# Latent attention entry: the last gate product behind three key and query tiles, its weights in a spent sum buffer, the key rotation on GpSimd, SiLUs ahead of the exponentials

## Chip, cores and metric

One Trainium2 chip, one of its NeuronCores. The metric is device time in microseconds (us) of one execution. The engines are named as in the profile: PE is TensorE, DVE is VectorE, ACT is ScalarE, POOL is GpSimd, SP is SyncE, which issues most transfers here.

## What is computed

Two layers on x of 512 tokens by 1024 columns, fp32. The first, which the change touches, is multi-head latent attention with a gate; the second is a sparse attention.

```
proj = rms_norm(x) @ w_in               # 1024 -> 384 + 256 + 64 + 2048
c_q, c_kv, k_pe, z = split(proj)
q  = rms_norm(c_q) @ w_uq               # 16 heads of 192
kv = rms_norm(c_kv) @ w_ukv             # 16 heads of 128 + 128
k  = concat(k_pe (shared), k_nope)
q, k = rope(rms_norm(q)), rope(rms_norm(k))    # first 64 columns rotate
o  = causal_attention(q, k, v)
x  = x + (o * silu(z)) @ w_out
```

## The kernel before

Each fp32 matmul is three fp32r ones: an operand is split into a high part (a copy by ACT, `w_hi`) and a low part (the difference, by DVE or POOL, `w_lo`), and PE forms hi·hi, lo·hi and hi·lo (`mm3`, L95 to L97). A PE weight tile can be used when both parts are there.

The five engines run written-out programs in order and meet only at semaphores, so each engine's order is exactly the order of its code.

**Gate products.** The gate path z (2048 columns) is computed in four chunks of 512 columns, each by seven half-size products in place of eight (sums of blocks on both sides, Strassen's scheme). They are numbered 0 to 27 here (`NB` = 28); product i is seven-step q = i // 7, block b = i % 7. For each, ACT makes `w_hi` (`block_hi`), DVE `w_lo` (`block_lo`, L1896) in a ring of four half buffers, PE runs 24 matmuls of 256 columns (`z_product`), and DVE adds the bank into z (`z_sums`). Some blocks are differences that DVE makes first (`w_difference`, L1912). ACT applies SiLU to the finished quarters (`z_leave`). The token side of blocks 1 to 3 are sums of h, in three buffers `h_sum`; each is last read by product 22, 23 or 24.

**Key rotation.** In the loop step after product 17 or so (`p == 18`), DVE scales and rotates the shared 64 key columns of all tokens (`keys_rotate`, L1960): eight small instructions, of which the last counts `kpe_step` to 4. SP waits for that before it loads the first head weights.

**Entry into the heads.** A tile is 128 tokens. `project_kv(m)` (6 matmuls of 256 columns) and `project_q(m)` (9 of 384) make keys with values, and queries of two heads, for tile m. The first head weights lie where ring places of products 24 and 25 were, the second where those of 26 and 27 were; they are split by `split_kv` and `split_q` on ACT and then DVE. PE's order is products 0 to 26, `project_kv(0)`, `project_q(0)`, product 27, then the slots.

**Slots.** From then on all engines run `step(s)` for s = -7 to 65. Slot s of PE holds `scores(s)`, `turn(s + 4)` (four transposes of normed keys and queries), `project_kv(s + 8)`, `values(s - 2)`, `turn_probs(s - 1)`, and a `project_q` in each of slots -8 to -5 and in every second slot from -2 on. Before tile m is turned, ACT squares it (`q_stats`, `kv_stats`), POOL makes the factors by a power (`k_factor`, `q_factor`), DVE scales (`scale_k`, `scale_q`) and rotates the first three tiles, POOL rotates the others (`rotate`). After it, ACT copies the high part (`high`) and DVE subtracts (`low`), which frees the bank (`x_free`). POOL first clears two parts of `qkT_lo`, after `z_used` has reached 28. In slot 0, ACT runs the first `exponential` and then the last pair of SiLUs.

## Time and profile before

| | |
|---|---|
| median of 3 runs | 944.73 us (943.12 to 945.89) |
| profiled execution, first to last instruction | 944.0 us |
| PE busy | 920.2 us (97%) |
| DVE, ACT, POOL busy | 557.2, 447.6, 413.8 us |

The profiled execution's time is given by its span alone. In the page PE is busy nearly all the time, so the idle time of the other engines matters only where PE waits for them, and the place to look is where PE is not busy.

### The profile page before, as it was taken

The page shows a single profiled execution, that of the slowest core. Times are in us where ns is not written, and L with a number is a line of the kernel's source. Part 1 is how long each engine was busy: PE and PEld are TensorE (multiplying, and loading weights), DVE is VectorE, ACT ScalarE, POOL GpSimd, SP SyncE. Part 2 cuts the span into 40 slices and gives each one's busy share as a digit, 9 for nine tenths or more (in the row PEclk, how much of TensorE's full clock was granted, in tenths as well). Part 3 has the DMA queues.
Part 4 walks back from the last instruction along what each step waited for, and adds up shares of the span by engine and source line. Part 5 has one row for each costly group of instructions (what it writes and reads, how often), then busy time and mean ns, then how long its engine had stood idle before and what let it go on. Part 6 is the DMA issues. An engine that isn't in the chain of part 4 may idle for free.

```text
span 944.0 us, 16372 instructions
## 1 busy us (share of the span) xinstructions
PE 920.2 (97%) x5910; PEld 824.9 (87%) x5910; DVE 557.2 (59%) x1665; ACT 447.6 (47%) x1019; POOL 413.8 (44%) x589
## 2 busy tenths in 40 slices
PE   6999997999999999999999999999999999999998
PEld 6999987999999998888888887888888999999986
DVE  5898867887788877211111125676946666666611
ACT  5456556877777777222342233444344333333310
POOL 2000118888888884133373335666713111111021
PEclk9999999999999999999999999999999999999999
DMA  6322412101111011213272122222120100000011
GB/s 203 116 90 90 126 38 92 49 12 49 48 39 48 24 47 47 86 50 120 84 155 104 58 76 89 90 95 88 53 84 5 42 1 1 1 1 1 2 38 52
DMA packets 39322, 58.91 MB, mean 62 GB/s; under 512 B 8757, under 2 KB 22346, under 8 KB 39242
## 3 DMA queue, kind: packets, MB, share of 16 engines
q1 hardware_dynamic: 39200, 57.85, 19.2%
q8 instruction: 48, 0.79, 0.3%
q14 instruction: 32, 0.26, 0.1%
q10 hardware_dynamic: 42, 0.01, 0.0%
HBM read 55.63 MB, written 2.10 MB: 61 GB/s over the span
## 4 chain that ended last, share of the span: by engine, by line
PE 81%; ACT 1%; DVE 0%; issue 0%; DVEq 0%
PE bank L95 16%; PE bank L96 15%; PE bank L97 15%; PE bank L533 7%; PE bank L1113 4%; PE bank L453 2%; PE bank L462 2%; PE bank L454 2%; PE bank L431 2%; PE bank L1102 2%; PE bank L1074 1%; PE bank L1075 1%; PE bank L1093 1%; PE bank L1092 1%; PE bank L469 1%; PE bank L518 1%
## 5 line engine op out<-in xcount | busy, mean ns | idle before, releaser
L1769 POOL TENSOR_TENSOR w_lo<-w_raw,w_hi 128x2048 fp32r<-128x2048 f32 (+1 forms) x26 | 118.3, 4549 | 148.6 <-ACT w_hi L1520 148.5
L95 PE MATMUL bank<-w_hi,h_hi 128*128 128x512 f32 (+3 forms) x480 | 172.9, 360 | 1.2 <-DVE h_lo L1816 0.9
L97 PE MATMUL bank<-w_hi,h_lo 128*128 128x512 f32 (+3 forms) x480 | 169.1, 352 | 0.0
L96 PE MATMUL bank<-w_lo,h_hi 128*128 128x512 f32 (+3 forms) x480 | 169.1, 352 | 0.0
L95 PEld LDWEIGHTS bank<-w_hi,h_hi 128*128 128x128 f32 x480 | 90.7, 189 | 13.9 <-issue 2.5
L97 PEld LDWEIGHTS bank<-w_hi,h_lo 128*128 128x128 f32 x480 | 90.6, 189 | 11.5
L96 PEld LDWEIGHTS bank<-w_lo,h_hi 128*128 128x128 f32 x480 | 90.7, 189 | 10.1
L1520 ACT ACTIVATE w_hi<-w_raw 128x2048 fp32r<-128x2048 f32 (+1 forms) x26 | 49.2, 1891 | 76.7 <-PE bank L97 76.7
L692 POOL TENSOR_TENSOR o_c<-o_c,o_sw 128x256 f32<-128x256 f32 x16 | 11.6, 727 | 167.2 <-DVE o_c L766 167.2
L533 PE MATMUL bank<-kvr,probT 128*128 128x65 f32 x640 | 80.7, 273 | 0.0
L95 PE MATMUL bank<-w_hi,c_hi 128*128 128x256 f32 (+1 forms) x224 | 76.9, 343 | 3.3 <-DVE w_lo L1991 0.9
L533 PEld LDWEIGHTS bank<-kvr,probT 128*128 128x128 f32 x640 | 78.6, 192 | 1.3
L95 PE MATMUL bank<-w_hi,o_hi 128*128 128x512 f32 x192 | 77.3, 403 | 0.0
L96 PE MATMUL bank<-w_lo,o_hi 128*128 128x512 f32 x192 | 75.8, 395 | 0.0
L97 PE MATMUL bank<-w_hi,o_lo 128*128 128x512 f32 x192 | 75.7, 394 | 0.0
L97 PE MATMUL bank<-w_hi,c_lo 128*128 128x256 f32 (+1 forms) x224 | 69.5, 310 | 0.0
L96 PE MATMUL bank<-w_lo,c_hi 128*128 128x256 f32 (+1 forms) x224 | 69.3, 309 | 0.0
L717 DVE CUSTOM_DVE_ANT_0 scored<-bank,band 128x128 f32<-128x128 f32 (+3 forms) x128 | 56.4, 487 | 18.6 <-PE bank L431 18.6
L636 ACT ACTIVATE probT<-bank 128x512 f32<-128x512 f32 (+1 forms) x96 | 47.0, 524 | 30.0 <-PE bank L469 29.1
L1470 ACT ACTIVATE qkT_hi<-bank 128x512 fp32r<-128x512 f32 x64 | 38.3, 599 | 30.9 <-PE bank L1075 30.8
L1730 POOL TENSOR_TENSOR ms_k<-ms_k,minus_half 128x1 f32<-128x1 f32 x64 | 46.0, 719 | 5.3
L1113 PE MATMUL bank<-kv_sb,probT 128*128 128x128 f32 x320 | 46.5, 276 | 1.3 <-DVE probT L2052 0.9
(312 smaller groups left out, 2390.0 us busy)
## 6 DMA issues: line engine op xcount, KB each, us to landing
w_raw<-in_nsa_w_in SPq DMA_DIRECT2D x10, 1024.0 KB, 4.9
w_raw<-in_mla_w_in SPq DMA_DIRECT2D x8, 1024.0 KB, 5.0
w_raw<-in_mla_w_out SPq DMA_DIRECT2D x8, 1024.0 KB, 5.0
w_raw<-in_nsa_w_in SPq DMA_DIRECT2D x8, 984.0 KB, 4.9
w_raw<-in_nsa_w_out SPq DMA_DIRECT2D x4, 1024.0 KB, 5.0
w_raw<-in_mla_w_uq SPq DMA_DIRECT2D x7, 576.0 KB, 4.1
w_raw<-in_mla_w_ukv SPq DMA_DIRECT2D x15, 256.0 KB, 2.6
w_raw<-in_mla_w_in SPq DMA_DIRECT2D x4, 704.0 KB, 5.7
```

The costliest lines, as they stand in the source:

```text
L95: nc.tensor.matmul(out, a[0], b[0], start=start, stop=False)
L96: nc.tensor.matmul(out, a[0], b[1], start=False, stop=False)
L97: return nc.tensor.matmul(out, a[1], b[0], start=False, stop=stop)
L431: nc.tensor.matmul(first_bank(k)[:, 0:nb * keys].rearrange("p (b c) -> p b c", b=nb), qT_hi[a][0:DK, tok], kT_hi[0:DK, b0:b0 + nb, n // HP ...
L533: last = nc.tensor.matmul(o_most[:, i, b, :] if i < 3 else o_last[:, b, :], probT[n % 2][:, at:at + P], kvr[:, j, c0:c0 + DV1], start=j == ...
L636: nc.scalar.activation(probT[n % 2][:, at:at + wide], score_bank[k % 3][:, 0:wide], ACT.Exp).then_inc(exp_done, 1)
L717: last = nc.vector.tensor_tensor_reduce(scored[k % 2][:, w * keys:(w + 1) * keys], first_bank(k)[:, w * keys:(w + 1) * keys], band[:, SEQ ...
L1113: last = nc.tensor.matmul(o_bank[:, 0:DV0], probT[:, i % 2, j * P:(j + 1) * P], kv_sb[:, h % 4 * NT + j, NOPE:WKV], start=j == 0, stop=j == i)
L1470: nc.scalar.activation(qkT_hi[m // NT % 2][:, :, t * P:(t + 1) * P], x_bank[m % 2][:, :].rearrange("p (a t) -> p a t", a=4), ACT.Copy).the ...
L1520: nc.scalar.activation(w_hi[g % 2][:, :, 0:width], w_raw[g % 2][:, :, 0:width], ACT.Copy).then_inc(m_hi, 1)
L1730: nc.gpsimd.tensor_tensor(at, at, minus_half[:, 0:1], ALU.pow).then_inc(k_factors, 1)
L1769: nc.gpsimd.tensor_tensor(w_lo[g % 2][:, :, 0:width], w_raw[g % 2][:, :, 0:width], w_hi[g % 2][:, :, 0:width].bitcast(F32), ALU.subtract). ...
```

## The change

Five edits, all around the entry.

- Product 27 runs after `project_kv` and `project_q` of tiles 0, 1 and 2. Its weights go into `h_sum[2]`, which product 24 was the last to read, and its result into bank 7; the first turn into bank 7, `turn(1)`, waits for its sum. The second head weights can then be split after product 26 in place of 27.
- `keys_rotate` moves from DVE to POOL, behind POOL's work on the latent factors.
- POOL clears `qkT_lo` after `z_used` has reached 23, not 28.
- ACT and DVE split the first head weights ahead of the SiLUs and sums of products 25 and later.
- The last SiLUs are run in slot -4, and a one-column Exp on a spare tile in slot -3 loads the Exp table there.

```diff
-z_bank = lambda i: bank[i % 4 if i < NB - 2 else (3, 2)[i - NB + 2]]
-bank_user = lambda i: i - 4 if i < NB - 2 else i - (3, 5)[i - NB + 2]
+z_bank = lambda i: bank[i % 4 if i < NB - 2 else (3, 7)[i - NB + 2]]
+bank_user = lambda i: i - 4 if i < NB - 2 else i - 3
+z_hi_at = lambda i: in_ring(w_hi, i) if i < NB - 1 else h_sum[2][0][:, :, :]
+z_lo_at = lambda i: in_ring(w_lo, i) if i < NB - 1 else h_sum[2][1][:, :, :]
...
 def turn(m):
+    if m == 1:
+        pe.wait_ge(z_sum, Z_STEPS * NZ)
...
 # PE
-    for q in range(NZ):
-        for b in range(7):
-            if 7 * q + b == NB - 1:
-                project_kv(0)
-                project_q(0)
-            z_product(q, b)
-    slots(step, KV0 + 1)
+    for i in range(NB - 1):
+        z_product(i // 7, i % 7)
+    project_kv(0)
+    project_q(0)
+    step(KV0 + 1)
+    step(KV0 + 2)
+    z_product(NZ - 1, 6)
+    slots(step, KV0 + 3)
...
 # ACT, split_q and split_kv
-    act.wait_ge(z_used, NB - 2 + 2 * p)
+    act.wait_ge(z_used, NB - 2 + p)
 # ACT, step
-    if s == 0:
+    if s == KV0 + 1:
+        z_leave(NB - 2)
+    if s == T0:
         z_leave(NB - 1)
+    if s == T0 + 1:
+        nc.scalar.activation(exp_junk[:, 0:1], minus_half[:, 0:1], ACT.Exp)
...
 # POOL
+    pool.wait_ge(gains_loaded, 16 * 6)
+    pool.wait_ge(tables_done, 1)
+    keys_rotate()
     pool.wait_ge(kpe_step, 4)
-    pool.wait_ge(z_used, NB)
+    pool.wait_ge(z_used, NB - 5)
...
 # DVE, after the loop over p
+    z_sums(NB - 4)
+    split_kv(0)
+    split_q(0)
+    z_sums(NB - 3)
+    z_sums(NB - 2)
+    split_kv(1)
+    block_lo(NB - 1)
+    split_q(1)
```

First place, PE at the entry. Each row shown begins one group (`c_hi` as input: a projection, 256 columns for keys, 384 for queries; `h_hi` as input: product 27). Before:

```order
L95 MATMUL bank5<-w_hi0,c_hi_57 128x256 [waits c_lo_made,wk_ready]
...
L95 MATMUL bank4<-w_hi0,c_hi_57 128x384 [waits c_lo_made,wq_ready]
...
L95 MATMUL bank2<-w_hi1,h_hi_68 128x256 [waits z_sum,z_lo]
...
L95 MATMUL bank1<-w_hi0,c_hi_57 128x256 [waits z_sum]
...
L95 MATMUL bank0<-w_hi0,c_hi_57 128x384 [waits z_sum]
...
L95 MATMUL bank5<-w_hi0,c_hi_57 128x256 [waits kv_out]
...
L95 MATMUL bank3<-w_hi0,c_hi_57 128x384 [waits z_sum]
...
L95 MATMUL bank1<-w_hi0,c_hi_57 128x256 [waits kv_out]
...
L95 MATMUL bank2<-w_hi0,c_hi_57 128x384 [waits z_sum]
...
L1074 MATMUL bank6<-ident,qn_70 128x128 [waits k_scaled,k_rotated,q_rotated]
```

and after:

```order
L95 MATMUL bank5<-w_hi0,c_hi_57 128x256 [waits c_lo_made,wk_ready]
...
L95 MATMUL bank4<-w_hi0,c_hi_57 128x384 [waits c_lo_made,wq_ready]
...
L95 MATMUL bank1<-w_hi0,c_hi_57 128x256 [waits z_sum]
...
L95 MATMUL bank0<-w_hi0,c_hi_57 128x384 [waits z_sum]
...
L95 MATMUL bank5<-w_hi0,c_hi_57 128x256 [waits kv_out]
...
L95 MATMUL bank3<-w_hi0,c_hi_57 128x384 [waits z_sum]
...
L95 MATMUL bank7<-h_sum_hi2_91,h_hi_69 128x256 [waits z_lo]
...
L95 MATMUL bank1<-w_hi0,c_hi_57 128x256 [waits kv_out]
...
L1079 MATMUL bank6<-ident,qn_71 128x128 [waits k_scaled,k_rotated,q_rotated]
```

Product 27 moved behind the projections of tiles 1 and 2, and reads `h_sum_hi` in place of the ring.

Second place, DVE at the entry (bank into `z_sb`: a sum; `w_lo0<-wh_first`: the first head weights; `w_lo1<-w_raw0`: the second). Before:

```order
L1928 TENSOR_TENSOR z_sb_56<-bank0,z_sb_56 128x2x256 [waits z_sum,z_used]
...
L1931 TENSOR_TENSOR z_sb_56<-bank1,z_sb_56 128x2x256 [waits z_used]
L1991 TENSOR_TENSOR w_lo0<-wh_first_97,w_hi0 128x512 [waits wk_hi_made]
L1986 TENSOR_TENSOR w_lo0<-wh_first_97,w_hi0 128x1152 [waits wq_hi_made]
L1934 TENSOR_TENSOR z_sb_56<-bank3,z_sb_56 128x2x256 [waits z_sum,z_used]
L1937 TENSOR_TENSOR z_sb_56<-bank2,z_sb_56 128x2x256 [waits z_sum,z_used]
...
L1991 TENSOR_TENSOR w_lo1<-w_raw0,w_hi1 128x512 [waits wk_hi_made,o_free]
L1986 TENSOR_TENSOR w_lo1<-w_raw0,w_hi1 128x1152 [waits wq_hi_made]
L2023 SCALAR_TENSOR_TENSOR kn_102<-kv_sb_71,ms_k_67,gk0 128x128 [waits k_factors,kv_out]
```

and after:

```order
L1958 TENSOR_TENSOR z_sb_56<-bank0,z_sb_56 128x2x256 [waits z_sum,z_used]
...
L2005 TENSOR_TENSOR w_lo0<-wh_first_98,w_hi0 128x512 [waits wk_hi_made]
L2000 TENSOR_TENSOR w_lo0<-wh_first_98,w_hi0 128x1152 [waits wq_hi_made]
L1961 TENSOR_TENSOR z_sb_56<-bank1,z_sb_56 128x2x256 [waits z_used]
L1964 TENSOR_TENSOR z_sb_56<-bank3,z_sb_56 128x2x256 [waits z_sum,z_used]
L2005 TENSOR_TENSOR w_lo1<-w_raw0,w_hi1 128x512 [waits wk_hi_made]
L1926 TENSOR_TENSOR h_sum_lo2_92<-w_diff_97,h_sum_hi2_91 128x1024 [waits z_hi]
L2000 TENSOR_TENSOR w_lo1<-w_raw0,w_hi1 128x1152 [waits wq_hi_made]
...
L2037 SCALAR_TENSOR_TENSOR kn_103<-kv_sb_72,ms_k_67,gk0 128x128 [waits k_factors,kv_out,o_free]
```

Both splits of the first head weights moved ahead of one sum, and those of the second ahead of tile 0's scaling but without the wait for product 27, whose own split stands between them.

Third place, ACT around the first exponential (`below` as input). Before:

```order
L1478 ACT_TABLE_LOAD
L1478 ACTIVATE prob_107,rowsum_64<-below0_105,negmax_63 128x128 [waits max_done]
L1378 ACT_TABLE_LOAD
L1378 ACTIVATE z_sb_56<-z_sb_56,ms_x_61 128x256 [waits z_sum]
...
L1470 ACTIVATE qkT_hi1_99<-bank7 128x4x128 [waits x_done]
...
L1478 ACT_TABLE_LOAD
L1478 ACTIVATE prob_107,rowsum_64<-below1_106,negmax_63 128x256 [waits max_done]
```

and after:

```order
L1384 ACTIVATE z_sb_56<-z_sb_56,ms_x_61 128x256 [waits z_sum]
...
L1476 ACTIVATE qkT_hi0_99<-bank7 128x4x128 [waits x_done]
...
L1514 ACT_TABLE_LOAD
L1514 ACTIVATE exp_junk_68<-minus_half 128x1
L1476 ACTIVATE qkT_hi0_99<-bank6 128x4x128 [waits x_done]
...
L1484 ACTIVATE prob_108,rowsum_64<-below0_106,negmax_63 128x128 [waits max_done]
...
L1476 ACTIVATE qkT_hi1_100<-bank7 128x4x128 [waits x_done]
...
L1484 ACTIVATE prob_108,rowsum_64<-below1_107,negmax_63 128x256 [waits max_done]
```

Of three table loads one is left, two turns further ahead, and the SiLUs stand before it.

## Rows read from the trace of the kernel before

**Rows 1.** Page, part 1: busy us, share of the span, instructions.
```profile
PE 920.2 (97%) x5910; PEld 824.9 (87%) x5910; DVE 557.2 (59%) x1665; ACT 447.6 (47%) x1019; POOL 413.8 (44%) x589
```

**Rows 2.** Stretches: busy (count) of PE, PEld, DVE, ACT, POOL; PEclk, DMA, GB/s.
```profile
132.00:136.00 4.00, 4.00 (x19) 4.00 (x19) 0.00 (x0) 2.21 (x9) 0.00 (x0) 0.58 0.00 0
...
152.00:156.00 4.00, 4.00 (x20) 3.90 (x18) 1.75 (x6) 2.13 (x7) 3.65 (x10) 0.57 0.00 2
...
172.00:229.00 57.00, 57.00 (x435) 55.79 (x434) 45.81 (x154) 44.09 (x148) 48.91 (x112) 1.00 0.13 40
```

**Rows 3.** Waits of PE from 172 us on: us in total, times, longest.
```profile
PE bank L1113 <- DVE probT L2052: 0.9, 2, 0.7
```

**Rows 4.** Timeline of PE, gate products: start, us, instruction, [idle before <-releaser].
```profile
112.81 0.39 PE L95 MATMUL bank<-w_hi,h_sum_hi 128*128 128x256 f32 x1 [0.23 <-DVE w_lo L1896]
...
119.90 0.39 PE L95 MATMUL bank<-w_hi,h_sum_hi 128*128 128x256 f32 x1 [0.44 <-DVE w_lo L1896]
```

**Rows 5.** Timeline of PE, entry into the heads.
```profile
129.65 0.39 PE L95 MATMUL bank<-w_hi,c_hi 128*128 128x256 f32 x1 [0.95 <-DVE w_lo L1991]
...
131.37 0.44 PE L95 MATMUL bank<-w_hi,c_hi 128*128 128x384 f32 x1 [0.75 <-DVE w_lo L1986]
...
132.07 0.52 PE L95 MATMUL bank<-w_hi,c_hi 128*128 128x384 f32 x1
...
138.32 0.34 PE L96 MATMUL bank<-w_lo,c_hi 128*128 128x384 f32 x1
138.50 0.34 PE L97 MATMUL bank<-w_hi,c_lo 128*128 128x384 f32 x1
```

**Rows 6.** Timeline of PE, turns and first slots.
```profile
144.94 0.33 PE L1074 MATMUL bank<-ident,qn 128*128 128x128 f32 x1 [0.46 <-DVE qn L2016]
...
147.43 0.33 PE L1074 MATMUL bank<-ident,qn 128*128 128x128 f32 x1 [1.12 <-DVE qn L2016]
...
151.33 0.30 PE L1074 MATMUL bank<-ident,qn 128*128 128x128 f32 x1 [2.53 <-DVE qkT_lo L2036]
...
159.47 0.44 PE L95 MATMUL bank<-w_hi,c_hi 128*128 128x384 f32 x1 [0.84 <-DVE qn L1998]
...
165.20 0.39 PE L95 MATMUL bank<-w_hi,c_hi 128*128 128x256 f32 x1 [0.74 <-ACT kv_sb L1464]
...
167.28 0.44 PE L1102 MATMUL bank<-ident,prob 128*128 128x128 f32 x2 [0.88 <-ACT prob L1478]
```

**Rows 7.** Timeline of VectorE: key rotation, a split, the first head split.
```profile
108.95 0.42 DVE L1963 TENSOR_TENSOR c_sb<-c_sb,gk 128x256 f32<-128x256 f32 x1
...
111.54 1.21 DVE L1896 TENSOR_TENSOR w_lo<-w_raw,w_hi 128x1024 fp32r<-128x1024 f32 x1
...
129.96 1.36 DVE L1986 TENSOR_TENSOR w_lo<-wh_first,w_hi 128x1152 fp32r<-128x1152 f32 x1 [0.36 <-ACT w_hi L1433]
```

**Rows 8.** Timeline of ScalarE: a split, the first head split, a table load.
```profile
109.13 1.06 ACT L1366 ACTIVATE w_hi<-w_raw 128x1024 fp32r<-128x1024 f32 x1 [2.14 <-DVE w_raw L1912]
...
128.26 0.61 ACT L1441 ACTIVATE w_hi<-wh_first 128x512 fp32r<-128x512 f32 x1
...
165.33 1.28 ACT L1478 ACT_TABLE_LOAD   x1
```

**Rows 9.** Timeline of GpSimd: clearing, factors, a rotation.
```profile
137.75 0.52 POOL L1714 MEMSET qkT_lo<- 64x512 f32 x1 [36.50 <-PE bank L97]
...
139.42 1.78 POOL L1730 TENSOR_TENSOR ms_k<-ms_k,minus_half 128x1 f32<-128x1 f32 x1
...
142.66 0.34 POOL L1729 TENSOR_SCALAR ms_k<-ms_k,ms_c,kpe_ms 128x1 f32<-128x1 f32 x1
...
145.04 0.45 POOL L1729 TENSOR_SCALAR ms_k<-ms_k,ms_c,kpe_ms 128x1 f32<-128x1 f32 x1
...
151.91 0.36 POOL L1746 TENSOR_TENSOR rotq<-qn,tcos 128x64 f32<-128x64 f32 x1 [0.34 <-DVE qn L1998]
...
154.17 0.34 POOL L1729 TENSOR_SCALAR ms_k<-ms_k,ms_c,kpe_ms 128x1 f32<-128x1 f32 x1
```

More of the change, by code:

```diff
@@ L178, in trunk @@
                 ms_k = place("ms_k", 21 * KB + 256, [P, NT])
+                exp_junk = place("exp_junk", 21 * KB + 320, [P, 8])
                 h_hi = place("h_hi", 22 * KB, [P, DM // P, SEQ], F32R)
@@ L1030, in project_q @@
                             pe.wait_ge(c_lo_made, KQ + KKV)
-                        if 0 < m < NT:
-                            pe.wait_ge(z_sum, Z_STEPS * NZ - (3, 1, 0)[m - 1])
+                        if 0 < m < NT - 1:
+                            pe.wait_ge(z_sum, Z_STEPS * NZ - (3, 1)[m - 1])
                         if m == NT:
@@ L1365, in block_hi @@
                             act.wait_ge(a_landed[1], 16 * (NCC + q + 1))
-                        nc.scalar.activation(in_ring(w_hi, i), w_block[b], ACT.Copy).then_inc(z_hi, 1)
+                        nc.scalar.activation(z_hi_at(i), w_block[b], ACT.Copy).then_inc(z_hi, 1)
                     def z_copy(q):
@@ L1642, in kc_high @@
                                              ACT.Copy).then_inc(kt_hi, 1)
-                    for p in range(NB + 1):
-                        if p == NB - 2:
-                            split_kv(0)
-                            split_q(0)
+                    for p in range(NB - 3):
                         if p % 7 == 1:
@@ L1652, in _ @@
                             sum_hi(3)
-                        block_hi(p + 3)
-                        if p == NB:
-                            kv_stats(0)
-                            q_stats(0)
-                            split_kv(1)
-                            split_q(1)
-                        elif p:
+                        if p + 3 < NB - 1:
+                            block_hi(p + 3)
+                        if p:
                             z_leave(p - 1)
@@ L1667, in _ @@
                                                  scale=g_c[:, k:k + 1]).then_inc(c_hi_made, 1)
-                    slots(step)
+                    block_hi(NB - 1)
+                    split_kv(0)
+                    split_q(0)
+                    z_leave(NB - 4)
+                    split_kv(1)
+                    kv_stats(0)
+                    split_q(1)
+                    q_stats(0)
+                    z_leave(NB - 3)
+                    slots(step, KV0 + 1)
                     first_high, attend = sparse_scalar(act)
@@ L1697, in lo, with keys_rotate @@
                                                 w_hi[g % 2][:, :, 0:width].bitcast(F32), ALU.subtract).then_inc(a_lo, 1)
+                    def keys_rotate():
+                        ok = Order(pool, kpe_step)
+                        pe_in = c_sb[:, :, CQ + CKV:CC]
+                        ok.link(nc.gpsimd.tensor_tensor(pe_in, pe_in, gk0[:, 0:ROPE].unsqueeze(1).to_broadcast([P, NT, ROPE]),
+                                                        ALU.mult))
+                        x1, x2 = pe_in[:, :, 0:HALF0], pe_in[:, :, HALF0:ROPE]
+                        cos, sin = tcos[:, 0:NT, 0:HALF0], tsin[:, 0:NT, 0:HALF0]
+                        nc.gpsimd.tensor_tensor(rot_pe[:, 0], x1, cos, ALU.mult)
+                        nc.gpsimd.tensor_tensor(rot_pe[:, 1], x2, sin, ALU.mult)
+                        nc.gpsimd.tensor_tensor(rot_pe[:, 2], x2, cos, ALU.mult)
+                        ok.link(nc.gpsimd.tensor_tensor(rot_pe[:, 3], x1, sin, ALU.mult))
+                        nc.gpsimd.tensor_tensor(kpe_sb[:, :, 0:HALF0], rot_pe[:, 0], rot_pe[:, 1], ALU.subtract)
+                        ok.link(nc.gpsimd.tensor_tensor(kpe_sb[:, :, HALF0:ROPE], rot_pe[:, 2], rot_pe[:, 3], ALU.add))
+                        nc.gpsimd.tensor_scalar(kpe_ms[:, :, 1:2], kpe_ms[:, :, 1:2], EPS, None, ALU.add).then_inc(kpe_step, 1)
                     lo(1)
@@ L1895, in block_lo @@
                         dve.wait_ge(z_hi, i + 1)
-                        nc.vector.tensor_tensor(in_ring(w_lo, i), w_block[i % 7], in_ring(w_hi, i).bitcast(F32),
+                        nc.vector.tensor_tensor(z_lo_at(i), w_block[i % 7], z_hi_at(i).bitcast(F32),
                                                 ALU.subtract).then_inc(z_lo, 1)
@@ L2072, in step @@
                             maximum(s)
+                        if s == KV0 + 3:
+                            z_sums(NB - 1)
                         if k_tile(s - 1) is not None:
@@ L2092, in step @@
                             o_low(s - SLOTS0 + 1)
-                    for p in range(NB + 1):
+                    for p in range(NB - 3):
                         if p:
                             z_sums(p - 1)
-                        if p == NB - 2:
-                            split_kv(0)
-                            split_q(0)
-                        block_lo(p + 3)
+                        if p + 3 < NB - 1:
+                            block_lo(p + 3)
                         w_difference(p + 4)
@@ L2103, in _ @@
                             c_low(LATENT_AT.index(p))
-                        if p == 18:
-                            dve.wait_ge(c_squared, 3 * NT)
-                            keys_rotate()
+                    z_sums(NB - 4)
+                    split_kv(0)
+                    split_q(0)
+                    z_sums(NB - 3)
+                    z_sums(NB - 2)
+                    split_kv(1)
+                    block_lo(NB - 1)
+                    split_q(1)
                     nc.vector.memset(rinv[:, :], 1.0).then_inc(o_free, 1)
                     dve.wait_ge(o_free, 1)
-                    split_kv(1)
-                    split_q(1)
-                    slots(step)
+                    slots(step, KV0 + 1)
                     def x1_leave(c):
```

27 lines of the change are left out of this document (6 added, 21 removed).

## Prediction

> **What bounds the kernel now.** I read the page's busy times first: PE is busy 920.2 of 944.0 us [rows 1], so at most some 24 us can be won without taking matmuls away, and the change takes none away. Then the stretches and PE's waits: from 172 us on PE is busy without a gap through the head slots (57.00 of 57.00 us [rows 2]) and its largest wait group is 0.9 us [rows 3]. What the change can win therefore lies before 172 us, and whatever it wins there moves everything behind it forward by as much. The timeline of PE has eleven places in the stretch 112 to 168 us where it stands still: three at gate products 22 to 24 (the first and the last are shown, the middle one is like the last) [rows 4], two at the entry into the heads [rows 5], one each before turns 0, 1 and 2, and three in the slots [rows 6].
>
> Two stretches are worse than they look. In 132 to 136 and in 152 to 156 us PE counts as busy for all 4 us, but the granted clock is 0.58 and 0.57 [rows 2], that is the lower level (1.2 GHz in place of 2.4) for most of each, and a matmul of 384 columns takes 0.52 us there against 0.34 [rows 5]. Both come right behind idle time: 0.95 and 0.75 us with little work between them [rows 5], and 0.46, 1.12 and 2.53 us [rows 6]. The waits of 0.84, 0.74 and 0.88 us later, spread over 8 us [rows 6], bring none.
>
> **The price of a wait.** The idle time in a row isn't all. The first matmul behind a wait is longer than the same one in a row (0.44 against 0.34 us for 384 columns [rows 5]) and the next begins later too; I count the idle time plus 0.15 us for each wait, an estimate from that pair.
>
> **1. Key rotation off DVE.** It runs there from 108.95 us to just before the sum ahead of the split at 111.54 [rows 7], about 2.0 us. The split at 111.54 could have begun when ACT's high part was done, at 109.13 + 1.06 = 110.19 [rows 8]. So the chain of difference, high part and low part, which hands products 22, 23 and 24 to PE, moves up by about 1.3 us. That chain needs 3.55 us a product (119.90 - 112.81 over two [rows 4]) where PE, without the wait of 0.44 and what hangs on it, needs about 2.9, so it wins product 22 and 23 their waits and leaves some 0.4 us at product 24. The three waits cost 0.23 + 2 × 0.44 + 3 × 0.15 = 1.56 us; **1.3 us** of it goes. On POOL the rotation costs more, but POOL has been idle there (36.50 us ahead of its clearing [rows 9]). POOL's nearest rows are 0.36 us for 64 columns [rows 9]; eight instructions of 128 or 256 columns are 3 to 5 us, from about 101 to 105 us, earlier than DVE ended (111). SP's load of the first head weights, which waits for it, starts earlier by that. Cost on the path: nothing. Bound on the other side: if POOL slowed DVE through shared memory access, DVE would lose at most the rotation's own 4 us around 103 us, and the wins of this step would be gone: 0 in place of 1.3.
>
> The Trainium skill, "GPSIMD Engine Reference", section 1 Specifications, says that GpSimd and VectorE share their SBUF interfaces and contend when VectorE reads two SBUF inputs, as its splits do. By that rule this step wins 0 and I'd say 1.3 less than below; POOL's factors at 142 to 156 us ran beside DVE at the pace that my sum uses, so what contention there is stands in those rows already.
>
> **2. Entry.** ACT's first head split starts at 128.26 us [rows 8], behind SiLUs that waited for DVE's sums, and DVE's follow; PE waits 0.95 and 0.75 us [rows 5], with 2 × 0.15 that is **2.0 us**. After the change ACT splits as soon as product 25 has been used, about 124.5 us on the new clock (1.3 earlier), 0.6 us and, by width, about 1.2 us long; DVE is through its sums by then, and has the key weights ready at 126.3 and the query weights at 127.6 (1.36 us for the latter [rows 7]). PE wants them at 127.2 and 127.9. Both waits go; the margin on the second is only 0.3 us.
>
> **3. First slow-clock stretch.** With those waits away PE runs on. The granted clock alone (0.58 over 4 us [rows 2]) means 4 × 0.42 = 1.7 us lost; by the matmuls (0.52 us in place of 0.34, some nine of them, all but the first few of 384 columns) it is 9 × 0.18 = 1.6 less what overlaps. I take **1.5 us**.
>
> **4. Turns.** Before, POOL started on tile 0 at about 138.8, after its two clearings, which had waited for product 27 (137.75 [rows 9]), and then the first power took 1.78 us [rows 9]. Tiles come out of POOL every 2.38 us (142.66 to 145.04 [rows 9]) and out of DVE every 2.49 us (147.43 - 144.94 [rows 6]), so turns 0, 1, 2 waited 0.46, 1.12 and 2.53 us [rows 6], with 3 × 0.15 it is 4.55 us. After the change POOL's clearing is long done and tile 0's squares come about 128.4, ten us earlier; but PE puts products and projections in between. PE: from 127.2 three pairs of projections of 2.3 us (9 matmuls of 384 columns, one every 0.18 us [rows 5], and 6 of 256 at two thirds of that), to 134.1, product 27 to 136.9, the fourth pair to 139.2, turn 0, keys 4, turn 1, keys 5: it wants turn 2 at 141.5. Vector side: POOL's first factors 131.1 and 132.1, DVE's second head split, product 27's split and the rotations of tiles 0 and 1 to 136.9, the sum of product 27 at 137.1 to 137.8 (it waits 0.25 for PE; tile 2's scaling queues behind it), tile 2 at 140.2. All three are ready in time. The new wait of turn 1 for that sum, with all of PE behind it, is met 2.5 us early. What is late next is the bank of turn 0: ACT's copy ends at 140.65 and DVE's three subtractions about 141.7, a wait of 0.25 + 0.15. Won: 4.55 - 0.4 = **4.15 us**.
>
> **5. Second slow-clock stretch.** Same as the first, **1.5 us**.
>
> **6. First slots.** The waits are 0.84 + 0.74 + 0.88 + 0.45 = 2.9 us [rows 6]. Two of their makers go: the table load at 165.33 us [rows 8], ahead of the exponential for which PE waited at 167.28, and the one before the SiLUs. A load costs 1.28 us of ACT; the one left is in slot -3 and delays only the copy of turn 2. But POOL isn't cured: from slot -4 it needs in two slots two key factors, a query factor and a rotation, 2.38 + 1.4 + 2.26 = 6.0 us (the last from 151.91 to 154.17 [rows 9]), and PE's two slots are only 3.9 to 5 us long until the scores grow wide. So PE, now without a slow clock, runs into POOL again at turns 3 and 4 and at queries 5 and 6. By the same addition that is some 0.2 + 0.6 + 0.85 + 0.15 us, 1.8 in all. Won: **1.1 us**.
>
> **Sum.** 1.3 + 2.0 + 1.5 + 4.15 + 1.5 + 1.1 = 11.55 us off the profiled 944.0 us, 932.45. The median of the runs lies 0.7 us above that span, so the time forecast is 933.2 us. The edits that move bank and buffer of product 27 cost nothing by themselves: 24 matmuls as before, and its split of 1.2 us moves behind DVE's second key split, ready 3 us ahead of PE.
>
> **Rivals.**
>
> *A slow stretch stays.* The remaining waits (0.4, then 1.8 us within 10) could still bring the clock down once. For it: PE idles right behind the turns, as before. Against it: 2.5 us of waits spread over 8 us brought nothing [rows 6]. Price 1.5 us, less what it hides of POOL's lateness: 934.7 us.
> The Trainium skill, "TensorE: Matmul & The Clock Gate", section "What's actually happening", says that where a transition falls varies from run to run of one kernel. By it a stretch may stay in some runs; the price is the one above.
>
> *The vector side is slower than its rows.* More work of DVE, ACT and POOL now lies side by side between 127 and 150 us. If DVE's instructions take a tenth longer, its chain to turn 2 (14 us of work) is 1.4 us late and again at turn 4: the win falls by about 3 us; a fifth longer, by about 7. For it: DVE has no slack in step 4 and the margin in step 2 is 0.3. Against: the rows it is made of were taken beside a POOL busy 3.65 of 4 us [rows 2]. Time 936.2 to 940.
>
> *The waits only move.* Product 27 behind tile 2 could be reached before DVE has split its weights, and turn 1 before its sum. The first 3 us of such lateness are covered; from there on each is a wait, and the slow clock comes back with it (3.0 us). It takes DVE 9 us later than I count to leave 11.55 - 6 - 3 = 2.5 us or less: 942 to 944, no change to tell.
>
> *Slower: the head slots lose their pace.* Slots 4 to 63 now begin with another spacing of POOL, ACT and DVE against PE. PE is full there, but POOL is busy 48.91 of 57 us [rows 2]; if the new spacing made PE wait in every slot, 60 slots would turn the win into a loss from 0.19 us a slot on; at 0.3 us it is 18 us, 951. Against it: each engine's order within a slot is unchanged, POOL has 8 us of slack in 57, and the old start, with POOL later still, settled to no wait at all [rows 2].
>
> **How the numbers follow.** Forecast 0.62; slow stretch stays 0.12; vector side slower 0.17; waits only move 0.05; slower 0.04. That the clock stays high and all waits of step 6 go as well is the better end of the forecast: 11.55 + 2.2 us off, 930.9. The range reaches from 930.8 to 938.0 and leaves out the last two and the worse end of the vector case. This kernel's measurement can tell 0.3%, 2.8 us, from no change. All cases but the last two are over that: faster 0.92, within 0.3% 0.04, slower 0.04.
>
> **What would show it.** PE's timeline without waits from product 22 to turn 1 except some 0.4 us at product 24; PE's clock at 1.00 in every 4 us stretch between 120 and 170; turn 2 within 0.5 us of when PE wants it; POOL idle from 106 to 128 us; one table load between the last SiLU and the first exponential; the two transposes of probabilities at 167.28 us before [rows 6] at about 155.7. It is wrong if a stretch with a clock near 0.6 is there, if product 27's first matmul waits, or if PE shows waits behind slot 8.

## The result, and the profile after

| | before | after |
|---|---|---|
| median of 4 runs | 945.29 us (943.12 to 945.89) | 934.69 us (934.23 to 935.11) |
| ratio, 95% interval | | 0.9893 (0.9881 to 0.9905) |
| profiled execution, first to last instruction | 944.0 us | 932.4 us (its time: 934.23 us) |

The forecast was 933.2 us, its range 930.8 to 938.0. The time lies 1.5 us above the forecast and inside the range; faster, as forecast, since the whole interval of the ratio lies below 1.

The page of the kernel after, busy us, share and instructions, beside [rows 1]:

```profile
PE 914.7 (98%) x5910; PEld 820.8 (88%) x5910; DVE 555.8 (60%) x1657; ACT 444.4 (48%) x1018; POOL 420.9 (45%) x597
```

DVE has lost eight instructions and POOL has gained eight, the key rotation. PE has the same 5910 matmuls in 5.5 us less busy time, though no work was taken away. Of that, 4.0 us lie between product 24 and the transposed probabilities of the second slot (39.11 us busy before, 35.11 after), where the two stretches at the lower clock were; 0.9 us lie ahead of the mark below, in work that the change doesn't touch. The stretches of the kernel after, columns as in [rows 2] (the last one is the head slots, twelve microseconds earlier than there):

```profile
140.00:144.00 4.00, 3.42 (x27) 3.25 (x27) 3.56 (x12) 3.98 (x11) 3.63 (x10) 1.00 0.00 2
144.00:148.00 4.00, 3.14 (x26) 2.73 (x24) 2.09 (x6) 3.77 (x15) 3.57 (x8) 1.00 0.00 0
148.00:152.00 4.00, 2.88 (x19) 2.68 (x18) 3.08 (x11) 1.84 (x7) 3.68 (x11) 1.00 0.68 213
...
160.00:217.00 57.00, 57.00 (x435) 55.80 (x434) 47.22 (x157) 44.06 (x147) 50.29 (x117) 1.00 0.13 41
```

The clock is 1.00 in each of these, also where PE still waits, and in the stretches from 112 to 140 us too. The timeline of PE, kernel after: a mark well ahead of the change (a projection of the latent stage that waits for its weights), then product 24, turns 0, 1, 2 and 4, query 5 and the second slot's transposed probabilities. It answers to [rows 4 to 6].

```profile
29.74 0.43 PE L95 MATMUL bank<-w_hi,h_hi 128*128 128x352 f32 x1 [0.31 <-DVE w_lo L1876]
...
118.21 0.39 PE L95 MATMUL bank<-w_hi,h_sum_hi 128*128 128x256 f32 x1 [0.44 <-DVE w_lo L1926]
...
138.92 0.27 PE L1079 MATMUL bank<-ident,qn 128*128 128x128 f32 x1
...
140.08 0.27 PE L1079 MATMUL bank<-ident,qn 128*128 128x128 f32 x1
...
141.95 0.30 PE L1079 MATMUL bank<-ident,qn 128*128 128x128 f32 x1 [0.57 <-DVE qkT_lo L2050]
...
147.49 0.30 PE L1079 MATMUL bank<-ident,qn 128*128 128x128 f32 x1 [0.86 <-DVE qkT_lo L2050]
...
150.09 0.44 PE L95 MATMUL bank<-w_hi,c_hi 128*128 128x384 f32 x1 [1.12 <-DVE qn L2012]
...
155.88 0.38 PE L1107 MATMUL bank<-ident,prob 128*128 128x128 f32 x2
```

Of eleven waits, four are left. The entry has none, and turns 0 and 1 have none.

The same mark in the kernel before:

```profile
30.33 0.43 PE L95 MATMUL bank<-w_hi,h_hi 128*128 128x352 f32 x1 [0.32 <-DVE w_lo L1846]
```

**A measure that holds still.** The profiled execution before had lost 0.59 us by that mark (30.33 - 29.74), long before anything that the change touches. It differs between executions of one kernel: the mark of the kernel after was at 29.74 in one profile and at 29.35 in another, whose spans, 932.4 and 932.0, differ by the same 0.4. From the mark to the two transposes at 155.88 (167.28 before [rows 6]) it is 126.14 us in the one and 126.11 in the other. I call this the *stretch*. Behind it every profile has 776.4 to 777.0 us. Before, the stretch was 136.95; so the change itself is worth **10.8 us** against this execution, which had two stretches at the lower clock. Of 33 other executions of the kernel before, about half have a mean clock that leaves room for only one (last section): against their median of 943.27 us the change wins 8.6 us, against the 945.30 us of the rest 10.6.

### The profile page after: what moved, and what is told of

It is laid out like the page before. It is cut to its first block, busy times and chain, and to the rows that moved or that the text cites. A ratio compares the mean times of both kernels' runs of the same rounds, so it can differ in the third digit from the quotient of the medians.

```text
span 932.4 us, 16370 instructions
## 1 busy us (share of the span) xinstructions
PE 914.7 (98%) x5910; PEld 820.8 (88%) x5910; DVE 555.8 (60%) x1657; ACT 444.4 (48%) x1018; POOL 420.9 (45%) x597
## 4 chain that ended last, share of the span: by engine, by line
PE 87%; DVE 6%; ACT 3%; issue 2%; POOL 1%; DMA 0%; ACTq 0%; DVEq 0%; POOLq 0%
PE bank L95 18%; PE bank L96 17%; PE bank L97 17%; PE bank L536 8%; PE bank L1118 4%; PE bank L456 2%; PE bank L465 2%; PE bank L434 2%; PE bank L457 2%; PE bank L1107 2%; DVE w_lo L1926 1%; PE bank L1079 1%; PE bank L1080 1%; ACT w_hi L1372 1%; PE bank L1098 1%
## 5 line engine op out<-in xcount | busy, mean ns | idle before, releaser
L95 PE MATMUL bank<-w_hi,h_hi 128*128 128x512 f32 (+3 forms) x472 | 170.4, 361 | 1.3 <-DVE h_lo L1846 1.0
L97 PE MATMUL bank<-w_hi,h_lo 128*128 128x512 f32 (+3 forms) x472 | 166.5, 353 | 0.0
L96 PE MATMUL bank<-w_lo,h_hi 128*128 128x512 f32 (+3 forms) x472 | 166.5, 353 | 0.0
L95 PEld LDWEIGHTS bank<-w_hi,h_hi 128*128 128x128 f32 x472 | 88.8, 188 | 14.1 <-issue 2.6
L97 PEld LDWEIGHTS bank<-w_hi,h_lo 128*128 128x128 f32 x472 | 88.7, 188 | 11.4
```

What stands on the lines that cost most here:

```text
L95: nc.tensor.matmul(out, a[0], b[0], start=start, stop=False)
L96: nc.tensor.matmul(out, a[0], b[1], start=False, stop=False)
L97: return nc.tensor.matmul(out, a[1], b[0], start=False, stop=stop)
```

## The experiments

"Ratio" is to the kernel before, with its 95% interval; the stretch is that of the profiled execution.

| kernel | median, us | ratio | stretch, us |
|---|---|---|---|
| before | 944.2 to 945.3 | 1 | 136.95 |
| after | 934.69 | 0.9893 (0.9881 to 0.9905) | 126.14 |
| after, again | 934.39 | 0.9899 (0.9883 to 0.9915) | 126.11 |
| keys on DVE | 935.54 | 0.9906 (0.9888 to 0.9924) | 127.28 |
| clearing late | 942.77 | 0.9978 (0.9969 to 0.9988) | 133.68 |
| spare POOL work | 936.40 | 0.9916 (0.9901 to 0.9931) | 127.33 |
| SiLUs late | 936.81 | 0.9919 (0.9905 to 0.9934) | 128.02 |
| splits late | 936.47 | 0.9914 (0.9898 to 0.9929) | 127.30 |
| product 27 first | 937.37 | 0.9925 (0.9908 to 0.9942) | 129.69 |
| product 27 behind four | 935.81 | 0.9911 (0.9894 to 0.9928) | 126.40 |
| before, clearing early | 941.45 | 0.9972 (0.9962 to 0.9983) | 133.53 |
| tile 3's rotation on DVE | 933.46 | 0.9884 (0.9869 to 0.9899) | 124.87 |
| the same, table load in slot 0 | 933.18 | 0.9885 (0.9870 to 0.9900) | 124.46 |
| the same, turn 0 subtracted first | 933.10 | 0.9887 (0.9869 to 0.9905) | 124.29 |

### Undoing one part

**Keys on DVE.** The `keys_rotate` of the kernel before in its old place; POOL does none of it.

```diff
+ if p == 18:
+     dve.wait_ge(c_squared, 3 * NT)
+     keys_rotate()          # nc.vector
```

> The changed kernel with the key rotation back on DVE, where it was; all else as changed. Theory (the rotation delayed the chain that hands products 22 to 24 to PE): waits ahead of those products come back, +1.1 to +1.3 us on the changed kernel's 934.7, so 935.8 to 936.0, and product 24 starts about 1.2 us later than 118.2. Rival (what DVE wins, shared access to SBUF with POOL takes back): no difference, 934.5 to 934.9.

The stretch is 1.14 us longer, all of it ahead of product 24 (119.85 against a mark at 30.25, that is 1.13 us later than in the kernel after), where two waits of 0.44 and 0.43 us stand. The entry has no wait in this kernel. The medians say 0.9 us, a little under the 1.1 to 1.3 expected. The theory holds; the rival, that shared access takes the gain back, falls.

**Clearing late.**

```diff
- pool.wait_ge(z_used, NB - 5)
+ pool.wait_ge(z_used, NB)
```

> The changed kernel with POOL's clearing waiting for z_used 28 again, that is for the end of product 27. Theory (POOL's late start on tile 0 made the waits of turns 0 to 2 and with them the second slow-clock stretch): turn 2 can't start before about 151 us, as in the kernel before, so PE waits some 9 us more before it and the clock falls; 942 to 946 us. Rival (POOL's start was covered, the entry's reordering alone won the time): within 1 us of the changed kernel, below 935.7.

PE's timeline at turns 0, 1 and 2, and its stretches from 140 to 156 us:

```profile
143.35 0.47 PE L1079 MATMUL bank<-ident,qn 128*128 128x128 f32 x1 [3.68 <-DVE qn L2030]
146.66 0.45 PE L1079 MATMUL bank<-ident,qn 128*128 128x128 f32 x1 [0.92 <-DVE z_sb L1967]
150.09 0.45 PE L1079 MATMUL bank<-ident,qn 128*128 128x128 f32 x1 [1.06 <-POOL kn L1762]
```

```profile
140.00:144.00 4.00, 0.65 (x3) 0.65 (x4) 3.03 (x12) 0.44 (x4) 3.60 (x10) 0.71 0.01 2
144.00:148.00 4.00, 3.08 (x16) 2.82 (x15) 3.86 (x16) 2.46 (x7) 3.60 (x9) 0.50 0.00 0
148.00:152.00 4.00, 2.94 (x14) 2.67 (x14) 3.67 (x13) 3.10 (x7) 3.04 (x9) 0.50 0.01 2
152.00:156.00 4.00, 4.00 (x19) 3.90 (x18) 1.94 (x5) 1.87 (x8) 3.57 (x8) 0.58 0.00 0
```

One constant costs 7.5 us of stretch, and the time is inside what was expected. PE's three waits make 5.66 us, where the kernel after has 2.55 in three; most of the rest is the low clock. PE stands 3.68 us for tile 0, whose factors POOL can't begin before 138.6, and then the granted clock is 0.50, the lower level, for eight microseconds, and low for part of the four on either side. In the third row the profile names POOL's `kn`, but that one (149.56 to 149.96) is tile 4's, and turn 2 needs those of tiles 0 to 2 only; the last thing that it waits for is the bank of turn 0, which DVE frees at 149.94.

**Splits late.** ACT: `z_leave(NB - 4)` ahead of the two splits; DVE: `z_sums(NB - 3)` ahead of them.

```diff
+ z_leave(NB - 4)            # ACT
  split_kv(0); split_q(0)
...
+ z_sums(NB - 3)             # DVE
  split_kv(0); split_q(0)
```

> The changed kernel with the first head weights' splits behind the SiLUs and sums of products 24 and 25, as before. Theory (this order made the entry's two waits): key weights are ready 1.0 to 1.3 us later than 126.0, PE waits 0.3 to 1.0 us at the entry, 935.2 to 936.0, clock still 1.00. Rival 1 (two edits together were needed, the other being the key rotation): no wait, 934.5 to 934.9. Rival 2 (the waits bring the slow clock back): a 4 us stretch at 0.6 near 132 us and 936.5 or more.

One wait at the entry is back:

```profile
129.35 0.45 PE L95 MATMUL bank<-w_hi,c_hi 128*128 128x384 f32 x1 [0.74 <-DVE w_lo L2000]
```

The stretch is 1.16 us longer, as expected; the query weights are late, and PE doesn't wait for the key weights. The median, 936.47, lies 0.5 us above the expected range. The clock stayed at 1.00 in the profile, and of the four executions one shows a mean clock of 0.998, the others 1.000.

**SiLUs late.**

```diff
- if s == T0: z_leave(NB - 1)
- if s == T0 + 1: nc.scalar.activation(exp_junk[:, 0:1], ..., ACT.Exp)
+ if s == 0: z_leave(NB - 1)
```

> The changed kernel with the last SiLUs in slot 0 again, behind the first exponential, and no early Exp. Theory (the table load ahead of the first exponential made the wait of 0.88 us before the first transposed probabilities): that wait is back near 156 us, 0.5 to 1.1 us, with 0.15 more behind it; 935.2 to 935.9. Rival (ACT is ahead of PE there by more than a load, or what the load costs is given back by turn 4, whose bank now comes 1.3 us sooner): within 0.3 us of the changed kernel's 934.7, or up to 0.4 less.

```profile
156.42 0.39 PE L95 MATMUL bank<-w_hi,c_hi 128*128 128x256 f32 x1 [0.61 <-ACT kv_sb L1470]
...
158.50 0.44 PE L1107 MATMUL bank<-ident,prob 128*128 128x128 f32 x2 [0.89 <-ACT prob L1484]
```

This cost 1.88 us of stretch, and the median of 936.81 lies above the expected 935.2 to 935.9: both last waits of [rows 6] are back, not only the second. The prediction had counted both (0.74 and 0.88); the expectation forgot the first. The run puts back the SiLUs and the two table loads around them together; which of them makes how much of it isn't taken apart.

**Product 27 first.** `z_product(NZ - 1, 6)` right behind the projections of tile 0.

> The changed kernel with product 27 right behind the projections of tile 0, ahead of those of tiles 1 and 2. Theory (the turns are met by POOL's early start, and the place of product 27 only gives DVE time for its split): PE waits about 1 us before product 27 (its low part is ready at 130.3, wanted at 129.3), part of it given back at turns 2 to 4; 935.0 to 935.9. Rival (the two extra tiles ahead of product 27 are what feeds POOL early): turns 0 to 2 wait 2 us or more together, and 937 us or more.

```profile
131.07 0.38 PE L95 MATMUL bank<-h_sum_hi,h_hi 128*128 128x256 f32 x1 [1.02 <-DVE h_sum_lo L1926]
...
144.85 0.30 PE L1079 MATMUL bank<-ident,qn 128*128 128x128 f32 x1 [1.47 <-POOL kn L1762]
...
153.00 0.69 PE L95 MATMUL bank<-w_hi,c_hi 128*128 128x384 f32 x1 [1.12 <-DVE qn L2012]
```

DVE in the same kernel, at the queries of tile 1 and at the end of its work on turn 0's bank:

```profile
138.36 0.74 DVE L2012 SCALAR_TENSOR_TENSOR qn<-bank,ms_q,gq 128x192 f32<-128x192 f32 x2 [1.31 <-POOL ms_q L1752]
...
144.42 0.28 DVE L2050 TENSOR_TENSOR qkT_lo<-bank,qkT_hi 64x128 fp32r<-64x128 f32 x1
```

The theory was half right, and the time is the rival's. Product 27 does wait 1.02 us for its weights, but nothing is given back: turn 2 waits 1.47 us (0.57 in the kernel after). The profile names POOL's `kn` as what ended the wait, but that one is tile 4's, and turn 2 doesn't need it. What turn 2 needs is the bank of turn 0, which DVE frees at 144.70, in the same moment. DVE is late there because it waited for POOL's factors of tile 1 (1.31 us), and POOL for that tile's squares: its projections now stand behind product 27. So tiles 1 and 2 ahead of product 27 do feed POOL earlier, which was the rival's point, though of the three turns only turn 2 waits, and less than the 2 us it named. In the profile the clock fell as well (0.58 from 152 to 156 us, the first matmul of query 5 takes 0.69 us); in the other three executions it didn't, and they took 937.0 to 937.5 us against this one's 938.7.

**Product 27 behind four tiles.**

> The changed kernel with product 27 behind four tiles, not three, and its sum one place later on DVE. Theory (POOL's lateness from tile 3 on makes the waits at turn 4 and query 5; it now gets tile 3's squares some 2.7 us sooner): those two shrink by 1 to 2 us, and turn 1 waits 0.3 to 1.0 us for the sum; 933.7 to 934.9. Rival (the bank of turn 1 is the tighter one): turn 1 waits 1.5 us or more and the whole is 935.5 or more.

```profile
142.60 0.30 PE L1079 MATMUL bank<-ident,qn 128*128 128x128 f32 x1 [0.68 <-DVE z_sb L1968]
...
149.34 0.30 PE L1079 MATMUL bank<-ident,qn 128*128 128x128 f32 x1 [0.87 <-DVE qkT_lo L2051]
...
151.94 0.45 PE L95 MATMUL bank<-w_hi,c_hi 128*128 128x384 f32 x1 [1.10 <-DVE qn L2013]
```

A miss. Turn 1 waits 0.68 us for the sum, as expected, but turn 4 and query 5 wait just as long as in the kernel after. POOL rotates tile 3 only behind the key factor of tile 4, whose squares come no sooner. The profile's stretch says 0.3 us worse; the median says 1.1, with 935.1 us twice and 936.5 and 937.0, so how much worse it is stays open. Nothing here speaks for four tiles.

### One part alone

**Before, clearing early.** The one constant of the change in the kernel before.

> The kernel before with one line of the change: POOL clears after z_used 23, not 28. Theory (POOL's start on tile 0 sets turns 0 to 2 there, 0.46, 1.12 and 2.53 us): tile 0 can start once its squares are there, some 2 us sooner, so the three waits shrink by 1.5 to 2.5 us; most of what the clearing cost shows only together with the two tiles put ahead of product 27. The entry's waits and the first slow stretch stay; the second goes or stays. 941.0 to 943.5. Rival (the clearing alone is the change's main gain, as its 8 us in the changed kernel suggest): 939 or less.

```profile
128.71 0.39 PE L95 MATMUL bank<-w_hi,c_hi 128*128 128x256 f32 x1 [0.94 <-DVE w_lo L1991]
...
130.43 0.45 PE L95 MATMUL bank<-w_hi,c_hi 128*128 128x384 f32 x1 [0.74 <-DVE w_lo L1986]
...
147.07 0.45 PE L1074 MATMUL bank<-ident,qn 128*128 128x128 f32 x1 [2.53 <-DVE qkT_lo L2036]
```

and POOL at the key factor of tile 1:

```profile
137.28 1.35 POOL L1729 TENSOR_SCALAR ms_k<-ms_k,ms_c,kpe_ms 128x1 f32<-128x1 f32 x1 [2.54 <-ACT sq_junk L1460]
```

The waits of turns 0 and 1 (0.46 and 1.12 [rows 6]) are gone; that of turn 2 is the same 2.53 us, for the bank of turn 0, which DVE frees only behind its work on the tiles that follow. The stretch is 3.4 us shorter, the median 2.8. Not all of it is the clearing's: the two waits that are gone make 1.9 us with 0.15 each, and the other 1.5 us are the stretch at the lower clock from 132 to 136 us, which this execution doesn't have though PE waited just as long ahead of it. Between executions of the same mean clock, 0.998, the median is 941.3 us here and 943.0 in the kernel before beside it, 1.7 us apart.

With *clearing late* this makes a cross of four kernels: neither 136.95, clearing alone 133.53, the other four edits alone 133.68, all five 126.14. Apart they are worth 3.4 us at most and 3.3, together 10.8. The clearing lets POOL start on tile 0 at 132.35. But in the old order it then waits 2.54 us for the squares of tile 1, whose projections stand behind product 27, and DVE scales tile 0 only from 138.23 on, behind product 27's sum and the split of the second head weights. The new order without the early clearing has the tiles ready and no POOL. The cross doesn't part the four edits from each other; of them the place of product 27 alone moves turn 2 by 2.2 us (*product 27 first*).

### The side effect on POOL

**Spare POOL work.** 20 products of 128 columns behind the key rotation, where POOL was idle.

```diff
+ for _ in range(5):
+     for r in range(4):
+         last = nc.gpsimd.tensor_tensor(rot_pe[:, r], kpe_sb[:, :, 0:HALF0], tcos[...], ALU.mult)
+     spare.link(last)
```

> The changed kernel with 20 spare products of 128 columns on POOL (one SBUF table times kpe, into a buffer that is spent) right behind the key rotation, where POOL was idle. Theory (POOL is held for as long as DVE reads two inputs from SBUF, DVE hardly loses): most spare products take 0.46 us, those that meet a split or difference of DVE 1.2 to 1.5 us; DVE's splits stay at 1.22 to 1.4 us; time within 0.4 us of the changed kernel, 934.3 to 935.1. Rival 1 (both sides are slowed alike): DVE's splits of 1.22 us take 1.5 us or more, product 24 starts 1 us later, 935.7 or more. Rival 2 (the length belongs to the instruction's place in its chain, not to DVE): all 20 take the same time within 0.1 us.

Timeline of DVE in this kernel (start, us), and of POOL in the same microseconds:

```profile
110.36 1.48 DVE L1931 TENSOR_TENSOR w_lo<-w_raw,w_hi 128x1024 fp32r<-128x1024 f32 x1 [0.58 <-ACT w_hi L1372]
111.76 1.48 DVE L1947 TENSOR_TENSOR w_diff<-w_raw 128x1024 f32<-128x1024 f32 x1
113.16 0.68 DVE L1969 TENSOR_TENSOR z_sb<-bank,z_sb 128x512 f32<-128x512 f32 x1
114.43 1.23 DVE L1931 TENSOR_TENSOR w_lo<-w_diff,w_hi 128x1024 fp32r<-128x1024 f32 x1 [0.59 <-ACT w_hi L1372]
```

```profile
110.29 0.47 POOL L1744 TENSOR_TENSOR rot_pe<-kpe_sb,tcos 128x128 f32<-128x128 f32 x1
110.83 1.32 POOL L1744 TENSOR_TENSOR rot_pe<-kpe_sb,tcos 128x128 f32<-128x128 f32 x1
112.12 1.44 POOL L1744 TENSOR_TENSOR rot_pe<-kpe_sb,tcos 128x128 f32<-128x128 f32 x1
113.52 0.46 POOL L1744 TENSOR_TENSOR rot_pe<-kpe_sb,tcos 128x128 f32<-128x128 f32 x1
113.94 0.46 POOL L1744 TENSOR_TENSOR rot_pe<-kpe_sb,tcos 128x128 f32<-128x128 f32 x1
114.47 1.50 POOL L1744 TENSOR_TENSOR rot_pe<-kpe_sb,tcos 128x128 f32<-128x128 f32 x1
```

One and the same product takes 0.46 us beside a sum from a bank (113.52, 113.94) and 1.32 to 1.50 beside a split or a difference, which reads two inputs from SBUF; it ends 0.3 us behind DVE's. The starts say the same as the lengths (110.83 to 112.12 is 1.29 us, 113.52 to 113.94 is 0.42). Nine of the 20 are long, eleven are 0.46 to 0.47. That was the theory's first half, and rival 2 falls. Its second half was too kind: a DVE instruction that starts while a product is running takes 1.48 in place of 1.22 us (110.36, 111.76), one that starts just ahead of it takes 1.23 (114.43). So each side waits for the other, by order of arrival, and DVE loses only the rest of a short product where POOL loses the whole of a long split. Those quarter microseconds sit in the chain of difference, high part and low part: from the mark, product 24 starts 0.8 us later, the first matmul on the query weights 1.1 us and turn 0 1.2 us, which is the whole of the stretch. That is rival 1's time with sizes nearer to the theory's.

The Trainium skill, "SBUF — State Buffer", section "Who interferes with whom", has the rule: a DVE instruction with two SBUF inputs and a GpSimd instruction that reads SBUF exclude each other, and whichever issues second is held until the first is through. The rows above agree in both directions; one case that doesn't, a split beside a power that had started first, stands in the last section.

### Better than both

What PE still waits for stands in the timeline of the kernel after: POOL comes to tile 3's rotation late, and ACT loads the Exp table for 1.28 us in slot -3 (142.93), ahead of the squares of tile 6. Three kernels, each with one edit more:

```diff
- if q_tile(s - 1) < NT - 1: rotate(q_tile(s - 1))     # DVE
+ if q_tile(s - 1) < NT: rotate(q_tile(s - 1))         # POOL: >= NT
```

> The changed kernel with the query rotation of tile 3 on DVE too (POOL starts with tile 4). Theory (POOL, with 6.0 us of work in two slots, makes the waits of 0.86 us at turn 4 and 1.12 us at query 5): both go or shrink, 0.6 to 2.3 us off, 933.4 as the middle. Rival (DVE is as full as POOL there, its rotation delays turn 3 and the freeing of the banks): waits move to turn 3 and the time is the same or up to 1 us longer, 934.7 to 935.7.

```diff
- if s == T0 + 1: nc.scalar.activation(exp_junk[:, 0:1], ..., ACT.Exp)
+ if s == 0: nc.scalar.activation(exp_junk[:, 0:1], ..., ACT.Exp)   # ahead of exponential(0)
```

> Tile 3's query rotation on DVE, and the early Exp moved from slot -3 to slot 0, right ahead of the first exponential, where ACT was idle for 1.07 us with DVE's maximum not yet there. Theory (the table load in slot -3 delays the squares of tile 6 by 1.3 us and through POOL query 5): the wait of 0.72 us at query 5 and 0.24 at turn 4 go, and the first exponential still ends before PE wants it at 152; 932.2 to 932.9. Rival (the exponential, now behind a load, is late for PE): a wait of 0.3 us or more before the first transposed probabilities, 933.3 or more.

```diff
+ if s == T0: low(0)                                   # DVE, moved ahead
  if k_tile(s - 1) is not None: scale_k(k_tile(s - 1))
```

> As the one before, and DVE's subtractions of turn 0 (low(0)) ahead of its scaling of the keys of tile 3. Theory (turn 2 waits for the bank of turn 0, 0.58 us, behind 0.35 us of key scaling): that wait is 0.3 us, 0.3 us less than the run before. Rival (ACT's copy isn't done when DVE comes to it, or tile 3 is late in turn): no difference, or 0.3 us more.

Turn 4 (in the first two; turn 3 has a small wait in its place) and query 5, PE's timelines of the first and the second kernel, and POOL's of the second:

```profile
144.94 0.30 PE L1079 MATMUL bank<-ident,qn 128*128 128x128 f32 x1 [0.24 <-DVE qkT_lo L2050]
...
148.67 0.44 PE L95 MATMUL bank<-w_hi,c_hi 128*128 128x384 f32 x1 [0.72 <-DVE qn L2012]
```

```profile
148.65 0.45 PE L95 MATMUL bank<-w_hi,c_hi 128*128 128x384 f32 x1 [0.29 <-DVE qn L2012]
```

```profile
146.39 1.43 POOL L1752 TENSOR_TENSOR ms_q<-ms_q,minus_half 128x2 f32<-128x2 f32 x1
```

POOL at the key factor of tile 6, in the kernel after and in the first of the three:

```profile
146.24 0.38 POOL L1759 TENSOR_SCALAR ms_k<-ms_k,ms_c,kpe_ms 128x1 f32<-128x1 f32 x1
```

```profile
145.09 0.34 POOL L1759 TENSOR_SCALAR ms_k<-ms_k,ms_c,kpe_ms 128x1 f32<-128x1 f32 x1 [0.93 <-ACT sq_junk L1466]
```

The first takes 1.27 us off the stretch: turn 4's wait of 0.86 is gone, turn 3 has one of 0.24, and query 5's falls from 1.12 to 0.72. Only now does the table load cost anything: in the kernel after, the squares of tile 6 are there at 145.16 and POOL, without a pause since tile 3's rotation, comes to them at 146.24; in the first of the three POOL stands 0.93 us for them. So the second, which moves the load, takes off 0.4 more, not the 0.9 expected: turn 3 still waits 0.25 us and query 5 0.29 us, since the power for its factor was held beside a split, 1.43 us against 0.70. The third takes off another 0.17; its edit did nothing for turn 2 (0.62 us in place of 0.57) and cost turn 3 0.3 us, but it shifted POOL so that the power was not held, and query 5 doesn't wait. That is luck of alignment, not the mechanism expected. The median of the last is 933.10 us (931.86 to 933.73), against 934.39 (933.82 to 935.09) of the changed kernel beside it: each of its four executions is below each of that one's. Between the last two the medians decide nothing.

## Why the prediction was right

The marks of the timelines cut the change into four pieces, each worked out as a difference of intervals, before minus after.

| from, to | steps | forecast | measured |
|---|---|---|---|
| mark, product 24 | 1 | 1.3 | 89.57 - 88.47 = 1.10 |
| product 24, turn 0 | 2, 3, wait of turn 0 | 2.0 + 1.5 + 0.6 = 4.1 | 25.04 - 20.71 = 4.33 |
| turn 0, turn 2 | 4 | 3.55 | 6.39 - 3.03 = 3.36 |
| turn 2, transposed probabilities | 5, 6 | 2.6 | 15.95 - 13.93 = 2.02 |
| sum | | 11.55 | 10.81 |

**Step 1** was right in mechanism: with the keys back on DVE 1.13 us return, so the contention that the prediction priced at the whole 1.3 us takes a fifth of it at most. The missing 0.2 us has two possible makers, which no run took apart. The prediction leaves some 0.4 us at product 24 (measured 0.44) and yet counts only 1.56 - 1.3 = 0.26 for it. And one split took 1.39 us for 1.21 because it met a product of POOL, shown here in the kernel after:

```profile
103.01 1.39 DVE L1926 TENSOR_TENSOR w_lo<-w_diff,w_hi 128x1024 fp32r<-128x1024 f32 x1
```

```profile
102.85 0.46 POOL L1719 TENSOR_TENSOR rot_pe<-c_sb,tsin 128x128 f32<-128x128 f32 x1
103.27 1.44 POOL L1720 TENSOR_TENSOR rot_pe<-c_sb,tcos 128x128 f32<-128x128 f32 x1
```

On POOL the rotation took 6.7 us, not 3 to 5: three of its eight instructions ran beside such DVE instructions. Its length cost nothing, since POOL was idle until its clearings at 115 us and again until 128.

**Steps 2 and 3** came out as forecast in size. *Splits late* gives back 1.2 of the 2.0 us, the wait for the query weights. The other wait, for the key weights, isn't the key rotation's: *keys on DVE* has no wait at the entry. What is left between *splits late* and the kernel before is product 27's split, which DVE did ahead of these sums and splits and now does behind the second head's key weights:

```profile
125.59 1.21 DVE L1896 TENSOR_TENSOR w_lo<-w_diff,w_hi 128x1024 fp32r<-128x1024 f32 x1
```

That its 1.2 us made the wait of 0.95 us is read from the order; no run put it back alone. The prediction says only that this split moves, and gives its effect to ACT's order. Step 3 holds for the profiled execution before; *before, clearing early* ran without that slow stretch behind the same two waits, so what step 3 wins differs from execution to execution, which the prediction left out.

**Step 4** was right: turn 2 waits 0.57 us for the bank of turn 0 where 0.25 was forecast, and turns 0 and 1 don't wait. The cross above shows that it needs the early clearing and the other edits at once.

**Steps 5 and 6**: the clock stayed, and the SiLUs and table loads were worth 1.9 us, as the two waits in the prediction say. What was off is the size of the rest: turn 4 and query 5 wait 0.86 and 1.12 us, with 0.15 each 2.3 us, where 1.8 was forecast over four places. The maker was named rightly (POOL; *tile 3's rotation on DVE* takes 1.27 us off), so the term that was too small is POOL's work from slot -4 on. The table load in slot -3, which was said to delay only the copy of turn 2, delays the squares of tile 6 too, but in the kernel after POOL comes to them later still; it costs 0.4 us only once tile 3's rotation is off POOL.

**One reading stopped short.** The prediction takes the first power's 1.78 us [rows 9] as a length of its own. A split with two SBUF inputs runs beside it in the kernel before, where most later powers of this size take 0.55 or 0.56 us:

```profile
139.42 1.36 DVE L1986 TENSOR_TENSOR w_lo<-w_raw,w_hi 128x1152 fp32r<-128x1152 f32 x1 [0.30 <-ACT w_hi L1433]
```

**Why the time was 1.5 us above the forecast.** No rival came true. The largest part, 1.1 us, is the last step of the sum, from span to time. I added 0.7 us, the median before less the profiled span. But each execution's time is 1.8 us above its own span (934.23 against 932.4), and the profiled execution before was one of the longer ones. The terms were 0.74 us too large. Against that, the profiled execution after reached the mark 0.59 us earlier and gained 0.2 behind the stretch; and the median lies 0.46 above that execution. With 1.8 in place of 0.7 the sum gives 934.25; that this meets the profiled 934.23 so closely is luck, two errors of nearly the same size.

**The rivals.** *A slow stretch stays*: not in any of 8 executions of the changed kernel, all at a mean clock of 1.000. It comes in some executions of its near relatives, one of four each with splits late, product 27 first, product 27 behind four tiles and spare POOL work. *Vector side slower*: seen in the small, one split of 1.39 for 1.21 us, and POOL's first three instructions on tile 0, 0.88, 1.44 and 1.01 us beside DVE's splits where later ones take 0.34, 0.56 and 0.40. Turn 0 doesn't wait for them. *Waits only move*: this is what the changed kernel does with the clearing late. *Slower*: PE is full from 160 to 217 us.

## What to carry to other kernels

When an engine is late at a point, look for both what it waits for and what it is fed: undoing the early clearing alone cost 7.5 of 10.8 us here, and undoing the other four edits and keeping it 7.4. Check the releaser that a row names against the semaphores that the instruction waits for: twice here it was another that ended in the same moment. Measure from a mark behind the first loads to one behind the change: two profiles of one kernel then agree within 0.03 us, where their spans differ by 0.4. Count an operation moved to an idle GpSimd with its price beside DVE's two-input instructions, not beside its neighbours in the trace, and place it where a quarter microsecond on DVE doesn't count.
